# Convolution in a two-block kernel: shifted rows by SyncE's transfers, three channel chunks summed in accumulation banks

## The reference

```python
CONV_WIDTH = 31
def depthwise_conv(u, w):
    return lax.conv_general_dilated(
        u, w[:, None, :].astype(u.dtype), window_strides=(1,),
        padding=[(CONV_WIDTH // 2, CONV_WIDTH // 2)],
        dimension_numbers=('NWC', 'WIO', 'NWC'), feature_group_count=u.shape[-1])

def conformer_conv(h, pw1_w, pw1_b, dw_w, dw_b, ln_g, ln_b, pw2_w, pw2_b):
    a, g = jnp.split(h @ pw1_w + pw1_b, 2, axis=-1)
    u = a * jax.nn.sigmoid(g)
    u = depthwise_conv(u, dw_w) + dw_b
    u = jax.nn.silu(layernorm(u, ln_g, ln_b))
    return u @ pw2_w + pw2_b
```

## Time and profile before

| | us |
|---|---|
| median of three runs | 1694.37 (1693.78 to 1695.69) |
| span of the profiled execution | 1694.2 |
| convolution stage in it, from VectorE's first tap to the mean | 1400.3 to 1457.3 |
| TensorE, VectorE, ACT, GpSimd busy over the span | 1657.7, 1173.1, 929.3, 765.9 |

### The profile page before, as it was taken

One profiled execution on the slowest core, in us unless ns is written; L12 is line 12 of the kernel. 1 busy time (PEld: TensorE's weight loads), 2 busy tenths in 40 slices (PEclk: granted clock), 3 DMA queues, 4 the chain that ended last, 5 costly groups with the idle time before them and its releaser, 6 DMA issues.

```text
span 1694.2 us, 31137 instructions
## 1 busy us (share of the span) xinstructions
PE 1657.7 (98%) x10730; PEld 1470.0 (87%) x10730; DVE 1173.1 (69%) x2096; ACT 929.3 (55%) x1523; POOL 765.9 (45%) x361
## 2 busy tenths in 40 slices
PE   8999999999999999999999999999999999999998
PEld 8778999988999998888888879958899988789997
DVE  4674289777777777778877786365655579675555
ACT  4474465587666665455454563264555564555554
POOL 4502668888999990000000014303455744235553
PEclk9999999999999999999999999999999999999999
DMA  6313565587555557888888862203555543145563
GB/s 235 102 38 120 168 210 178 183 292 258 181 177 178 168 171 260 291 286 286 290 293 286 288 227 96 97 1 125 172 186 184 184 150 119 61 153 188 186 185 123
DMA packets 86343, 312.39 MB, mean 184 GB/s; under 512 B 9842, under 2 KB 9842, under 8 KB 86130
## 3 DMA queue, kind: packets, MB, share of 16 engines
q1 hardware_dynamic: 85972, 309.38, 54.2%
q0 software_dynamic: 288, 1.97, 0.3%
HBM read 310.26 MB, written 1.05 MB: 184 GB/s over the span
## 4 chain that ended last, share of the span: by engine, by line
PE 84%; DVE 7%; ACT 3%; issue 3%; POOL 1%; DVEq 0%; DMA 0%; SPq 0%; ACTq 0%; POOLq 0%
PE psr L900 17%; PE psr L840 16%; PE psr L1169 10%; PE acc_all L1169 10%; PE psr L903 9%; PE acc_all L840 7%; PE psr L1116 3%; PE psr L787 1%; DVE arena L2585 1%; DVE wl L573 1%; POOL wl L573 1%; ACT wh L564 1%; PE psr L828 1%; PE psr L935 1%; PE psr L1048 1%
## 5 line engine op out<-in xcount | busy, mean ns | idle before, releaser
L573 POOL TENSOR_TENSOR wl<-ring,wh 128x1024 fp32r<-128x1024 f32 x280 | 684.0, 2445 | 548.3 <-ACT wh L564 532.0
L564 ACT ACTIVATE wh<-ring 128x1024 fp32r<-128x1024 f32 x474 | 498.9, 1054 | 307.0 <-PE psr L840 159.1
L900 PE MATMUL psr<-hb,wh 128*128 128x512 f32 x1344 | 343.5, 397 | 0.7 <-DVE hb L2002 0.7
L573 DVE TENSOR_TENSOR wl<-ring,wh 128x1024 fp32r<-128x1024 f32 x194 | 240.3, 1239 | 61.2 <-ACT wh L564 60.1
L900 PEld LDWEIGHTS psr<-hb,wh 128*128 128x128 f32 x1344 | 240.8, 189 | 45.5 <-DVE hb L2002 2.2
L840 PE MATMUL psr<-hb,wh 128*128 128x256 f32 (+1 forms) x1664 | 222.4, 286 | 5.9 <-DVE hb L1999 3.7
L840 PEld LDWEIGHTS psr<-hb,wh 128*128 128x128 f32 (+1 forms) x1664 | 209.1, 192 | 10.3 <-DVE hb L1999 4.5
L903 PEld LDWEIGHTS psr<-hb,wl 128*128 128x128 f32 x1344 | 182.7, 190 | 15.9 <-DVE wl L573 1.7
L1169 PE MATMUL psr<-wh,hb 128*128 128x512 f32 x504 | 196.1, 389 | 0.0
L1169 PE MATMUL acc_all<-wh,hb 128*128 128x512 f32 x504 | 196.1, 389 | 0.0
L903 PE MATMUL psr<-hb,wl 128*128 128x256 f32 x1344 | 187.7, 282 | 1.0 <-DVE wl L573 0.8
(11 more groups left out here) (375 smaller groups left out, 2709.9 us busy)
## 6 DMA issues: line engine op xcount, KB each, us to landing
ring<-in_peer_u SPq DMA_DIRECT2D x128, 512.0 KB, 3.5
ring<-in_peer_v SPq DMA_DIRECT2D x128, 512.0 KB, 5.0
sq<-in_ada_w SPq DMA_DIRECT2D x91, 512.0 KB, 4.0
ring<-in_ffn_a SPq DMA_DIRECT2D x44, 512.0 KB, 4.0
ring<-in_ffn_b SPq DMA_DIRECT2D x44, 512.0 KB, 3.4
ring<-in_ffn_d SPq DMA_DIRECT2D x44, 512.0 KB, 3.5
ring<-in_pw SPq DMA_DIRECT2D x24, 512.0 KB, 3.5
ring<-in_w_in SPq DMA_DIRECT2D x18, 512.0 KB, 3.4
```

The costliest lines, as they stand in the source:

```text
L564: nc.scalar.activation(wh[:, q % 2, :], ring[:, s, :], ACT.Copy).then_inc(high_ready, 1)
L573: eng.tensor_tensor(wl[:, q % 2, :], ring[:, n % NS, :], wh[:, q % 2, :], ALU.subtract)\
L900: mm(ps[:, :], wh[:, b, chunk(k)], hb[:, k, :, :], start=(k == 0), stop=False, skip_group_check=True)
```

## The change

- `conv_order()` becomes plain: all pw1 chunks, then the five packed convolutions, then the mean. The matmuls of `replicas` on TensorE and the moves on ACT go.
- SyncE makes the copies: for each of the five chunks 16 transfers from `upad` to `rep`, 32 partitions of 284 numbers (1136 bytes) each, behind a wait for the chunk's gate. They stand in SyncE's order behind the loads of pw1 tile 15 (chunk 3), pw2 tile 0 (chunk 4), pw2 tile 1 (chunk 5) and pw2 tile 3 (chunks 6 and 7). `packed_conv` waits for all 16 of its chunk. `rep` now has room for five chunks.
- VectorE's sums of chunks 0 to 2 are kept in `acc[0..2]` (PSUM) from the first tap to the last but one; the last tap of each writes `cv` in SBUF, and the third of them raises `conv_sum` in place of the nop.
- The gates of chunks 4 to 7 stand behind taps 3, 7, 11 and 15, where before it was 2, 4, 7 and 11.
- The stage's buffers lie at the start of the arena.

The diff, without the renamed order in `plan_groups` and what only drops calls:

```diff
@@ conv_order
-    order = [("pw1", c) for c in range(PE_CONV[0] + 3)]
-    for c in PE_CONV[:-1]:
-        order += [("rep", c)] + ([("pw1", c + 3)] if c + 3 < KC else [])
-        if c > PE_CONV[0]:
-            order.append(("conv", c - 1))
-    return order + [("rep", PE_CONV[-1]), ("conv", PE_CONV[-2]), ("conv", PE_CONV[-1]), ("mean", 0)]
+    return [("pw1", c) for c in range(KC)] + [("conv", c) for c in PE_CONV] + [("mean", 0)]
@@ buffers and semaphores
-                  ("diag", len(PE_CONV) * TAPG * P), ("rep", 2 * 4 * REPW)], base=c2n + 4096)
+                  ("diag", len(PE_CONV) * TAPG * P), ("rep", len(PE_CONV) * 4 * REPW)])
-        rep_made, rep_moved = sem("rep_made"), sem("rep_moved")
+        copies_in = [sem(f"copies_in{c}") for c in PE_CONV]
@@ SyncE
+            def copies(c):
+
+                drained(sp, ("pw1", c))
+                for b in range(4):
+                    for r in range(4):
+                        sp.dma_start(rep[32 * r:32 * r + 32, PE_CONV.index(c), b, :],
+                                     upad[32 * b:32 * b + 32, c, r:r + REPW]).then_inc(copies_in[PE_CONV.index(c)], 16)
+
+            copies_behind = {TILE_NO["pw1", 15]: PE_CONV[0:1], TILE_NO["pw2", 0]: PE_CONV[1:2], TILE_NO["pw2", 1]: PE_CONV[2:3],
+                             TILE_NO["pw2", 3]: PE_CONV[3:]}
...
                     load(n)
+                    for c in copies_behind.get(n, ()):
+                        copies(c)
@@ TensorE
-            def replicas(c):
-                n = PE_CONV.index(c)
-                drained(pe, ("pw1", c))
-                if n == 0:
-                    pe.wait_ge(gated_raw, 2)
-                for b in range(4):
-                    if n:
-                        pe.wait_ge(rep_moved, 4 * (n - 1) + b + 1)
-                    for r in range(4):
-                        last = mm(acc[b][32 * r:32 * r + 32, 0:REPW], ident[:, 32 * b:32 * b + 32],
-                                  upad[:, c, r:r + REPW], start=True, stop=True, skip_group_check=True)
-                    last.then_inc(rep_made, 1)
@@ packed_conv
-                pe.wait_ge(rep_moved, 4 * (n + 1))
+                pe.wait_ge(copies_in[n], 16 * 16)
@@ ScalarE
-            def replicas(c):
-                n = PE_CONV.index(c)
-                if n >= 2:
-                    full(act, ("conv", c - 2))
-                for b in range(4):
-                    act.wait_ge(rep_made, 4 * n + b + 1)
-                    A(rep[:, n % 2, b, :], acc[b][:, 0:REPW], ACT.Copy).then_inc(rep_moved, 1)
@@ VectorE
+            cv_sum = [acc[c][:, 0:T] for c in chunks]
-                        STT(out=cv[:, c, :], in0=upad[:, c, bass.ds(k, T)], scalar=dw[:, bass.ds(k + c * CONV, 1)],
-                            in1=cv[:, c, :], op0=ALU.mult, op1=ALU.add).then_inc(dve_step, 1)
+                        STT(out=cv_sum[c], in0=upad[:, c, bass.ds(k, T)], scalar=dw[:, bass.ds(k + c * CONV, 1)],
+                            in1=cv_sum[c], op0=ALU.mult, op1=ALU.add).then_inc(dve_step, 1)
-                TS(cv[:, c, :], upad[:, c, 0:T], dw[:, c * CONV:c * CONV + 1], par("dw_b")[:, c:c + 1],
+                TS(cv_sum[c], upad[:, c, 0:T], dw[:, c * CONV:c * CONV + 1], par("dw_b")[:, c:c + 1],
                    ALU.mult, ALU.add).then_inc(dve_step, 1)
-            taps = (1, 1, 3, 5, 8, 12, CONV)
+            taps = (1, 1, 4, 8, 12, 16, CONV - 1)
-            dve.wait_ge(dve_step, st.n)
-            nc.vector.nop().then_inc(conv_sum, 1)
+            for i, c in enumerate(chunks):
+                dve.wait_ge(dve_step, st.n - len(chunks) + i + 1)
+                ins = STT(out=cv[:, c, :], in0=upad[:, c, CONV - 1:CONV - 1 + T], scalar=dw[:, (c + 1) * CONV - 1:(c + 1) * CONV],
+                          in1=cv_sum[c], op0=ALU.mult, op1=ALU.add)
+            ins.then_inc(conv_sum, 1)
```

More of the change, by code:

```diff
@@ L191, in plan_groups @@
     g.append(("norm", 9))
-    g += [(what, c) for what, c in conv_order() if what != "rep" and (what, c) not in (("pw1", 0), ("pw1", 1))]
+    g += [(what, c) for what, c in conv_order() if (what, c) not in (("pw1", 0), ("pw1", 1))]
     g += [("norm", 10)] + [("pw2", c) for c in range(4)]
@@ L452, in build @@
         a4 = cut([("up", KC * UPW), ("cv", 2048), ("cv2", 2048), ("xc", 2048), ("sig", 512),
-                  ("diag", len(PE_CONV) * TAPG * P), ("rep", 2 * 4 * REPW)], base=c2n + 4096)
+                  ("diag", len(PE_CONV) * TAPG * P), ("rep", len(PE_CONV) * 4 * REPW)])
+        assert 6 * 1024 + 2304 + 512 + len(PE_CONV) * (TAPG * P + 4 * REPW) <= 22240
         upad = a4["up"].rearrange("p (c n) -> p c n", c=KC)
@@ L458, in build @@
         diag = a4["diag"].rearrange("p (c k n) -> p c k n", k=TAPG, n=P)
-        rep = a4["rep"].rearrange("p (h b n) -> p h b n", h=2, b=4)
+        rep = a4["rep"].rearrange("p (h b n) -> p h b n", h=len(PE_CONV), b=4)
         csig = a4["sig"].rearrange("p (b t) -> p b t", b=2)
@@ L1363, in packed_conv @@
                         last = mm(ps[32 * b:32 * b + 32, 0:T], diag[:, n, k, 32 * b:32 * b + 32],
-                                  rep[:, n % 2, b, 4 * k:4 * k + T], start=(k == 0), stop=(k == TAPG - 1),
+                                  rep[:, n, b, 4 * k:4 * k + T], start=(k == 0), stop=(k == TAPG - 1),
                                   skip_group_check=True)
@@ L1381, in _ @@
                     split_features("pw1", c, [(("pw1", c), h_parts)], turn=4 if c == 2 else None)
-                elif what == "rep":
-                    replicas(c)
                 elif what == "mean":
```

## The result

| | before | changed |
|---|---|---|
| median, us | 1694.07 (4 runs, 1693.42 to 1695.69) | 1712.49 (4 runs, 1709.91 to 1714.39) |
| ratio of the runs | 1 | 1.0108, 95% interval 1.0095 to 1.0121 |
| span of the profiled execution | 1694.2 | 1708.1 (its own time 1709.91) |
| first tap to centring in it | 1400.32 to 1457.31: 57.0 | 1396.48 to 1471.24: 74.8 |
| centring to the end of the span | 236.9 | 236.9 |

The change costs 18.4 us by the medians. All of it lies in the stage: that grew by 17.8 us and what follows it is as long as before. (The changed kernel came to the stage 3.8 us earlier in its profiled execution. Two stretches of low granted clock further up, where the change touches nothing, were half as long in it, and a third wasn't there.

The account below looks back on a forecast made before the run. VectorE was taken to bound the stage, TensorE one microsecond behind; afterwards SyncE's copies decide. Later mean +2.0, with ACT's lost cover +2.4, with 0.7 for the clock +3.1: 1697.5 us, range 1688.0 to 1701.5.

Parts of the forecast that it names:

- 83 steps of issuing: SyncE, first to 84th issue (80 copies, four loads): 0.475 us each, 39.4 us, the last issued at 1451.0.
- last convolution, with the clock: TensorE, chunk 7's packed convolution after its rows land: 3.55 us, plus 0.7 for a lowered granted clock.
- behind it to centring: After TensorE's last convolution: ACT's drain of 0.47 us, then 8 mean matmuls of 2.0 us, centring near 1459.3.
- ScalarE's cover in front of the squares: ACT's splits and table load after its last drain lose their 2 us cover; squares start at 1460.5, raising +2.0 to +2.4.
- Issue cost: SyncE, one transfer's issue, start to start: taken as 0.475 us from loads, independent of bytes; lower end 0.37.
- the likely case: SyncE issues at 0.475 us with little clock loss on TensorE: +1 to +5 us, chance 0.42.
- The mean: TensorE, end of the stage: only 8 of the mean's 16 matmuls follow the last convolution, 2.0 us.
- The clock: TensorE, gaps of 4 to 5 us before chunks 5, 6 and 7 lower its granted clock: 0.7 us.
- falls and stays: Rival: TensorE's clock drops in the gap before chunk 7 and stays low: +7 us, 1701.3, chance 0.16.
- VectorE sets the end: Rival: copies issue faster than 0.35 us, so VectorE's end at 1444 decides the stage: -11.6 us, 1682.8, chance 0.06.
- Held sums: Rival: VectorE stays held despite sums in banks, ending near 1455; under 1 us more, chance 0.03.
- Slow issues: Rival: SyncE issues up to 0.78 us apart, as beside heavy loads; last landing 1478.5, +27 us, chance 0.03.

Follow-up runs that it names:

- The kernel with the stores ahead: Changed kernel with rows sent through HBM, each store issued before the wait for the previous one and all before pw2 tiles 0 to 3: 1681.60 us, ratio 0.9933.
- either half alone: Kernel before with only VectorE's sums moved to banks: 1696.27 us; rows through HBM, stores ahead of waits and pw2 loads, sums kept in SBUF: 1695.23 us.

## Why the prediction was wrong, point by point

The forecast was a stage of 60.1 us (57.0 + 3.1); it took 74.8. By the prediction's own terms, each measured from the first tap:

| term | predicted | measured | difference |
|---|---|---|---|
| first copy issued after the first tap | 11.3 | 11.2 | -0.1 |
| 83 steps of issuing | 39.4 | 52.7 | +13.3 |
| last issue to the convolution's start | 2.2 | 2.0 | -0.2 |
| last convolution, with the clock | 4.3 | 5.1 | +0.8 |
| behind it to centring | 2.5 | 3.8 | +1.3 |
| ScalarE's cover in front of the squares | 0.4 | 0 | -0.4 |

- **Issue cost: the step that failed.** The mechanism was right: SyncE's issuing decides, the rows of chunks 4 to 7 come too late, the last one sets the end. The size was off, 0.475 in place of 0.635. The rows it was read from were all loads from HBM; the copies have both sides in SBUF, and no row of before showed such a transfer. The text asked whether bytes or the number of rows change the cost and didn't ask about the two sides. Its upper end for the likely case was its own value, and 0.78 was set aside as a matter of heavy loads, with a chance of 0.03; an unseen kind of transfer should have had a bound above 0.475. 83 x 0.16 is 13.3 us, nearly the whole error of 14.7. The 512 cycles of the Trainium skill, "DMA: Bandwidth & Descriptors", section "Why a DMA increments its semaphore by 16 and not by 1", an estimated 0.43 us, agree with the issues that have one side in HBM (0.42 to 0.46 here) and not with SBUF to SBUF (0.59).
- **The mean.** The text let 8 of the 16 matmuls run before the last convolution. They stand behind all convolutions in TensorE's order, so all 16 follow: 1.3 us more.
- **The clock.** Taken at 0.7, measured at 1.5 for the last convolution (5.18 against 3.66). The granted clock fell ahead of all four convolutions that follow a gap, and came back to 1.00 before each of them ended (at 1435, 1445, 1456 and 1466 it was there again); the rival "falls and stays" (+7) didn't happen.
- **VectorE: right to a few tenths.** Gates 4 to 7 were predicted at 1409, 1414.8, 1420.5 and 1425.7; less the 3.8 us by which the stage began earlier they came within 0.1 of that (1405.23, 1410.99, 1416.75, 1421.85). End predicted at 1444, measured 1439.95 + 3.8. A sum with a bank costs 0.391 us from start to start (42 from 1422.25 to 1438.69), and 0.396 with all in SBUF (42 from 1435.18 to 1451.80 in the kernel with the sums back in SBUF); the extra 62 cycles of the Trainium skill, "VectorE: DVE Perf Modes", section "The TRN2 errata — SBUF-src ops pay a fixed extra latency per instruction", don't show in this case, as the earlier trace rows had it.
- **TensorE: right.** pw1 was to end at 1425.0; chunk 3's convolution started at 1420.81 + 3.8.
- **The rivals.** "VectorE sets the end" named -11.6 us as what is there once the rows come in time. The kernel with the stores ahead has a stage 11.5 us shorter than before, but that the two agree is partly luck: TensorE sets the end there, by half a microsecond. Nor does the rival's own condition hold together: at 0.35 an issue the last convolution would end at 1446.4, behind VectorE's 1444. "Held sums" is refuted by the timelines. "Slow issues" came nearest (0.78 apart and +27, against 0.635 and +17.8), with the wrong condition: no heavy load is needed.

## What to carry to other kernels

When work moves to an issuing queue, count the issues, multiply by the cost of that kind of transfer (both ends, not size), and compare with the time in which they are wanted; where the trace has no transfer of that kind, keep the bound open upward. If the copies can't be made in few issues, going through HBM with larger transfers can be quicker than many small ones inside SBUF; here it was so only with the stores ahead of the waits and of the heavy loads. Two engines that end within a microsecond of each other have to be relieved together: here either half alone gave nothing and both, with the rows by way of HBM, gave 12.7 us.

## What the runs showed of the hardware

- An issue on SyncE's queue took 0.59 us from SBUF to SBUF and 0.42 to 0.46 with one side in HBM, in a row of its own kind, whether for 32 or 128 rows, and from SBUF to SBUF also for 16 or 1136 bytes a row.
- SyncE's and ScalarE's queues issued side by side at 0.592 and 0.620 us (medians).
- All 19 issues of SyncE and ScalarE that took over 1.0 us (up to 2.02) overlap a 16 KB packet on the instruction queue. With 36 idle matmuls a gap there were four such packets beside the copies, in the changed kernel two.
- A store of one chunk to HBM took 2.8 to 6.2 us to land, the longest behind 512 KB loads, and 1.7 to 4.1 with these moved behind it; the loads back took 2.4 to 4.7.
- With its sum in a bank VectorE wasn't held beside GpSimd's low parts (twelve sums in 4.79 us); with both tensors in SBUF it was (nine in 14.00).
- In gaps of some 5 us TensorE's granted clock fell each time, and a convolution of 3.66 us took 5.1 to 6.0.
